# A two-layer streaming trunk on one core: the first wait of the value normalisation moved, a sixth norm buffer, and the last attention head reordered

## The chip, the cores and the metric

One core of one Trainium2 chip. The time is device microseconds for one launch, as the median of several runs. One further execution was taken with the hardware profiler; every row below is from it.

## The reference

Two layers, each `h = x + RMSNorm_post(mixer(RMSNorm_pre(x)))`, over 1024 prompt tokens and 32 sample tokens (1056 together), width 1024, all in float32.

```python
def gmlp_branch(u, v, z, ws, bs, gv):                       # layer 0, branch A
    u = gelu(u)
    v = rmsnorm(gelu(v).reshape(b, L, 4, 256), gv)          # per token and group of 256
    s = einsum('gij,bcjgk->bcigk', masked(ws), v chunks of 128) + bs
    return silu(z) * u * s, v
# layer 0, branch B: a Mamba-2 SSD scan over 16 heads; its output is normalised too
# layer 0 out: concat(A, B) @ w_out (2048 x 1024)
def odd_layer(...):                                         # layer 1, attention, 8 heads of 128
    q, k, v, z, f_logit = split(h @ w_in)
    q, k = rmsnorm(q, gq), rmsnorm(k, gk)                   # per head, over its 128 features
    p = softmax(q @ k.T * scale + f_cum(q) - f_cum(k))      # causal; the sample rows also see 256 cached keys
    o = (silu(z) * (p @ v)) @ w_out                         # 1024 x 1024
    return x + rmsnorm(o, g_post)
```

## The kernel before

Activations are kept with features on the 128 partitions and tokens along the free axis, in three chunks of `CH` = 352. Every float32 product of the projections is made as three matrix products of split numbers: high x high, low x high, high x low. The high part is made by ScalarE (ACT: `split_high`, `out_high`), the low part is raw minus high, by GpSimd (POOL: `split_low`) or VectorE (DVE). TensorE (PE) works through one fixed list of products. All five queues are written out by hand and joined by semaphores (`S("name")`), so an engine does its list in order, and a wait at the head of a list holds all that stands behind it.

**Value tiles (layer 0, branch A).** `v_group(i)`, four times, projects two tiles of v, and turns them (transposes by PE) into banks `PB[3]` to `PB[7]`, and the sixth piece again into `PB[3]`, which is why PE there waits for `v_tok` from DVE's first copy out of `PB[3]`. DVE copies the six pieces to `V`, sums squares (`SQV`), normalises, and between adds up the squares of the SSD output `YB` in `RSY`. Ahead of the first of these, DVE waits for outputs of the scan to be stored by DMA (`ssd_stored`, `conv_stored`), clears part of `V` and `RSY`, and waits for the gains (`gv_in`).

**Attention (layer 1).** `turn_steps(t)` has 12 steps. In step i PE projects one chunk of head p = t + 1 (v, z, q, k in this order) and does a part of the attention of head t: `scores(i)`, `turn_probs(i-1)`, `values(i-2)` for query block i. DVE takes the row maximum with the bias (`sm`), ACT takes the exponential (`ex`), DVE divides (`pn`, written to `SB`), PE turns `SB`, ACT copies it to `PT`. The norms of q and k go by chunk n = 0 to 5 (three of q, three of k): POOL squares into `NRM`, ACT makes `NRMH`, DVE makes `NRML`, PE sums over partitions (`norm_sum`), DVE takes the mean (`n_ms`), ACT the inverse root (`inverse_root`), DVE multiplies (`norms`, `n_done`). `NRM` has five slots; chunk 5 uses slot 0 again (`NORM_SLOT`), so its squares wait for the norms of chunks 0 to 3.

**Last head.** `turn_steps(7, project=False)` has nothing left to project. Its steps carry products of the output projection instead (`fill(i)`): `FILL[i]` gives which group of three half rows and how many of the eight weight rows k, each with three products for each of the three half rows. Step 5 ends group 0, so that ACT then squares its three banks (`out_squares`) and DVE multiplies them by the gains (`out_gained`) and frees them; `fill(6)` starts group 1 in the same banks. Step 8 and `fill(9)` do the same for groups 1 and 2. k = 7 needs this head's own output, split by `last_head_high` (ACT) and `last_head_low` (DVE). Six of the output weights are loaded while it runs, into `WOR`, and split into `WOH` by ACT and `WOL` by POOL. After step 11 nine more half rows follow.

Of the kernel before, what the change touches and what calls it, by code (L numbers as in the profile page):

```python
# [2550 lines left out]
```

## Time and profile before

| | us |
|---|---|
| median of 3 runs | 1603.23 (1602.16 to 1603.6) |
| the profiled execution | 1603.08 |
| its span, first to last instruction | 1601.1 |
| PE busy in the span | 1546.9 |
| DVE, ACT, POOL busy | 794.6, 676.4, 442.3 |

PE is the engine that is nearly always busy; 54 us of the span are not covered by its matrix products. A time in a row is counted from the start of the span. A busy PE need not run at full speed: the granted clock is shown beside it in views by stretch, 1.00 being 2.4 GHz and 0.50 being 1.2 GHz.

### The profile page before, as it was taken

How to read it: one execution, taken by the hardware profiler on the slowest of the kernel's cores; microseconds unless marked ns; L12 is line 12 of the kernel's file. 1: busy time of each engine (PE TensorE's matmuls, PEld its weight loads, DVE VectorE, ACT ScalarE, POOL GpSimd, SP SyncE). 2: the span in 40 equal slices, each digit the busy share in tenths (PEclk: the TensorE clock that was granted, in tenths of full speed). 3: DMA queues.
4: the chain of work that ended last, by engine and by line, in shares of the span. 5: the costliest groups of instructions: out<-in, count | busy, mean ns of one | idle time of the engine just before them, and what ended most of it. 6: DMA issues, size and time to landing. Idle time of an engine off the chain costs nothing.

```text
span 1601.1 us, 26475 instructions
## 1 busy us (share of the span) xinstructions
PE 1546.9 (97%) x9472; PEld 1420.5 (89%) x9472; DVE 794.6 (50%) x1750; ACT 676.4 (42%) x1258; POOL 442.3 (28%) x269
## 2 busy tenths in 40 slices
PE   6999999998999999999999999999999999998898
PEld 5999999998999999988888898989889898986676
DVE  5546777776784232436565243434434343435432
ACT  6434444442233323335455344545444544445321
POOL 1214544452221112244442312222222121316000
PEclk9999999999999999999999999999999999999999
DMA  4122122203112111244555644724232332213121
GB/s 152 42 69 72 60 87 74 71 33 83 52 27 56 40 39 39 95 168 157 171 189 110 76 64 41 73 40 70 40 70 44 59 60 43 60 43 139 54 95 70
DMA packets 129510, 121.09 MB, mean 76 GB/s; under 512 B 10291, under 2 KB 113293, under 8 KB 129453
## 3 DMA queue, kind: packets, MB, share of 16 engines
q1 hardware_dynamic: 129452, 120.32, 31.0%
q8 instruction: 37, 0.61, 0.2%
q14 instruction: 21, 0.16, 0.0%
HBM read 101.64 MB, written 18.66 MB: 75 GB/s over the span
## 4 chain that ended last, share of the span: by engine, by line
PE 83%; DVE 5%; ACT 4%; issue 4%; DMA 2%; POOL 1%; SPq 0%; ACTq 0%; POOLq 0%; DVEq 0%
PE PB L747 78%; PE PB L751 5%; DVE NRML L1914 2%; DMA XT<-in_x_prompt_dram 1%; DMA WRAW<-in_w_in_odd_dram 1%; ACT L1328 1%; ACT L1793 1%; DVE SB L1918 0%; ACT SB L1877 0%; ACT PT L1322 0%; ACT NRMH L1322 0%; ACT SQJ L1362 0%; POOL WL L627 0%; DVE KALL L1921 0%; DVE XT L1921 0%
## 5 line engine op out<-in xcount | busy, mean ns | idle before, releaser
L747 PE MATMUL PB<-HH,WH 128*128 128x352 f32 x1872 | 619.5, 331 | 2.5 <-DVE HL L1914 1.6
L747 PE MATMUL PB<-HH,WL 128*128 128x352 f32 x1872 | 602.7, 322 | 0.0
L747 PE MATMUL PB<-HL,WH 128*128 128x352 f32 x1872 | 602.0, 322 | 0.0
L747 PEld LDWEIGHTS PB<-HH,WH 128*128 128x128 f32 x1872 | 352.8, 188 | 19.5 <-issue 12.5
L747 PEld LDWEIGHTS PB<-HL,WH 128*128 128x128 f32 x1872 | 353.9, 189 | 0.2
L747 PEld LDWEIGHTS PB<-HH,WL 128*128 128x128 f32 x1872 | 352.5, 188 | 0.0
L627 POOL TENSOR_TENSOR WL<-WRAW,WH 128x1024 fp32r<-128x1024 f32 x82 | 201.6, 2459 | 542.7 <-ACT WH L1322 536.0
L1322 ACT ACTIVATE WH<-WRAW 128x1024 fp32r<-128x1024 f32 x112 | 118.0, 1053 | 16.2 <-DMA WRAW<-in_w_out_even_dram 8.0
L1877 ACT ACTIVATE SB<-SB,small 128x128 f32<-128x128 f32 (+8 forms) x72 | 53.8, 748 | 80.0 <-DVE small L1918 80.0
L1914 DVE TENSOR_TENSOR Y<-PB,Y 128x128 f32 (+2 forms) x72 | 20.2, 280 | 133.1 <-PE PB L747 133.1
L747 PE MATMUL PB<-PT,VTOK 128*128 128x128 f32 (+2 forms) x624 | 81.6, 274 | 0.1
L747 PEld LDWEIGHTS PB<-PT,VTOK 128*128 128x128 f32 (+1 forms) x624 | 78.2, 191 | 1.6 <-issue 0.2
L747 PE MATMUL PB<-KALL,QT 128*128 128x512 f32 (+4 forms) x208 | 78.6, 485 | 0.0
L1914 DVE TENSOR_TENSOR NRML<-NRM,NRMH 128x352 fp32r<-128x352 f32 x48 | 47.2, 983 | 57.2 <-ACT NRMH L1322 57.2
L655 POOL TENSOR_TENSOR M<-M,CBT 128x512 f32<-128x512 f32 (+1 forms) x48 | 62.2, 1322 | 47.5 <-ACT M L1511 47.5
L747 PE MATMUL PB<-WH,YSH 128*128 128x512 f32 x192 | 75.1, 391 | 0.0
L747 PE MATMUL PB<-WL,YSH 128*128 128x512 f32 x192 | 74.8, 389 | 0.0
L1322 ACT ACTIVATE PT<-PB 128x512 f32<-128x512 f32 (+3 forms) x112 | 45.7, 446 | 62.4 <-PE PB L751 62.3
L679 POOL TENSOR_TENSOR WL<-WRAW,WH 128x512 fp32r<-128x512 f32 x30 | 53.5, 1785 | 63.1 <-ACT WH L1322 63.1
L747 PE MATMUL PB<-WH,YSL 128*128 128x512 f32 x172 | 66.9, 389 | 0.0
L1914 DVE TENSOR_TENSOR UG<-UG,ZG 128x1056 f32<-128x1056 f32 x8 | 12.2, 1528 | 105.5 <-ACT ZG L1342 105.5
L2420 DVE CUSTOM_DVE_ANT_0 SB<-PB,NFB 128x512 f32<-128x512 f32 (+4 forms) x104 | 54.5, 547 | 14.9 <-PE PB L751 7.7
(312 smaller groups left out, 2338.0 us busy)
## 6 DMA issues: line engine op xcount, KB each, us to landing
WRAW<-in_w_out_even_dram SPq DMA_DIRECT2D x48, 512.0 KB, 3.6
WRAW<-in_w_in_even_dram SPq DMA_DIRECT2D x44, 512.0 KB, 3.8
WRAW<-in_w_in_odd_dram SPq DMA_DIRECT2D x32, 512.0 KB, 8.0
ACSB<-acs_rows SPq DMA_DIRECT2D x16, 528.0 KB, 5.3
NFB<-nf_rows SPq DMA_DIRECT2D x8, 656.0 KB, 3.9
XS<-in_x_prompt_dram SPq DMA_DIRECT2D x8, 512.0 KB, 6.4
XT<-in_x_prompt_dram SPq DMA_DIRECT2D x8, 512.0 KB, 5.3
x_rows<-OG SPq DMA_DIRECT2D x8, 512.0 KB, 5.7
```

Source lines behind the costliest of these rows:

```text
L627: pool.tensor_tensor(WL[:, slot(w), :, :], WRAW[:, slot(w), :, :], WH[:, slot(w), :, :].bitcast(f32), ALU.subtract).then_inc(S("w_low"), 1)
L655: pool.tensor_tensor(m, m, CBT[0:rows, g, b0:b0 + nb, 0:rows], ALU.mult).then_inc(S("m"), 1)
L679: pool.tensor_tensor(WLS[SLOT3[u % 3]][:, HALF:D], raw[:, HALF:D], WHS[SLOT3[u % 3]][:, HALF:D].bitcast(f32), ALU.subtract).then_inc(S("w_ ...
L747: return pe.matmul(out, lhsT, rhs, start=start, stop=stop)
L751: return pe.transpose(out, in_, IDENT[0:n, 0:n])
L1322: return act.activation(out, in_, ACT.Copy, scale=scale)
L1328: act.add_instruction(mybir.InstLoadActFuncSet(name=nc.get_next_instruction_name(), act_func_set_id=LN_EXP_SET, ins=[], outs=[]))
L1793: act.activation(Y1[:, p, :], Y1[:, p, :], ACT.Silu).then_inc(S("zs"), 1)
L1877: act.activation(SB[0:rows, 0:width], SB[0:rows, 0:width], ACT.Exp, scale=SCALE, bias=NBIAS[0:rows, :], accum_out=RSUM[0:rows, :]).then_in ...
L1914: return dve.tensor_tensor(out, a, b, op)
L2420: order(dve.tensor_tensor_reduce(SB[0:rows, c0:c1], PB[3 + k][0:rows, 0:c1 - c0], NFB[0:rows, key0 + c0:key0 + c1], 1.0, -3.0e38, ALU.add, ...
```

## The change

Nothing that is computed changes, and no product is added or taken away. There are three parts.

1. On DVE, ahead of the first value group: the waits for the stored outputs and the clearing of `RSY` move behind that group's sums of squares, and the wait for the gains stands just ahead of their first use. What is left ahead of the copies is the wait for `yb` and the clearing of part of `V`. The loop over the groups is partly written out.
2. `NRM` and `NRML` get a sixth slot, which lies over `KC` (the cached keys), so the squares of chunk 5 wait for `kc_turn` (PE's turn of `KC`, step 10). In step 9 PE's `norm_sum` of chunk 2 stands behind `values`. In step 10 ACT's `NRMH` copy stands ahead of the inverse root.
3. In the last head `fill` leads every step; the last head's output is split one step earlier; in steps 5 and 8 ACT's three squares stand ahead of the exponential, and DVE's first two gains and the mean stand ahead of the maximum of the scores, the third ahead of the division. The low part of the second output weight is made by DVE, not POOL. POOL makes three low parts of `WOL`, waits for the norms of head 7 (`n_done` 16), makes the low part of head 6, and then the other three.

```diff
-    NRM = r("NRM", [P, 5, CH])
-    NRML = at("NRML", c_phase, [P, 5, CH], f32r)
+    KC = at("KC", c_phase + 5 * CH * 4, [P, 2, P])
+    KSAM = KC[0:DEC, 0, :]
+    NRM = r("NRM", [P, 6, CH])
+    NRML = at("NRML", c_phase, [P, 6, CH], f32r)
...
-    NORM_SLOT = (0, 1, 2, 3, 4, 0)
...
-        def turn_parts(p):
+        def turn_parts(p, last=False):
...
                 if n == 5:
-                    pool.wait_ge(S("n_done"), 2 * p + 1)
+                    pool.wait_ge(S("kc_turn"), p + 1)
                 for cols, src in norm_chunk(n):
-                    last = pool.tensor_tensor(NRM[:, NORM_SLOT[n], cols], src, src, ALU.mult)
+                    last = pool.tensor_tensor(NRM[:, n, cols], src, src, ALU.mult)
                 last.then_inc(S("n_sq"), 1)
...
-            split_low(tile_no(W_QKVZ + 4 + Z_, 4, p))
+            if not last:
+                split_low(tile_no(W_QKVZ + 4 + Z_, 4, p))
 
         turn_parts(0)
-        with pool.Fori(1, 8) as p:
-            turn_parts(p)
-            pool.wait_ge(S("y1_hi"), p)
-            pool.tensor_tensor(YL[:, p - 1, :], Y1[:, p - 1, :], YH[:, p - 1, :].bitcast(f32), ALU.subtract) \
+        def low_of_head(h):
+
+            pool.wait_ge(S("y1_hi"), h + 1)
+            pool.tensor_tensor(YL[:, h, :], Y1[:, h, :], YH[:, h, :].bitcast(f32), ALU.subtract) \
                 .then_inc(S("y1_lo"), 1)
-        for k in range(2, 8):
+
+        def out_low(k):
+
             pool.wait_ge(S("w_high"), W_OO + k + 1)
             pool.tensor_tensor(WOL[:, k - 2, :], WOR[:, k - 2, :], WOH[:, k - 2, :].bitcast(f32),
                                ALU.subtract).then_inc(S("w_low"), 1)
-            if k == 7:
-                pool.wait_ge(S("n_done"), 16)
-                pool.wait_ge(S("y1_lo"), 7)
-                pool.tensor_copy(YSAM[:, 0:7, 0:DEC], YH[:, 0:7, SEQ:TOK]).then_inc(S("ysam"), 1)
-                pool.tensor_copy(YSAM[:, 0:7, DEC:2 * DEC], YL[:, 0:7, SEQ:TOK]).then_inc(S("ysam"), 1)
+
+        with pool.Fori(1, 7) as p:
+            turn_parts(p)
+            low_of_head(p - 1)
+        turn_parts(7, last=True)
+        pool.wait_ge(S("w_low"), W_OO + 2)
+        for k in range(2, 5):
+            out_low(k)
+        pool.wait_ge(S("n_done"), 16)
+        low_of_head(6)
+        for k in range(5, 8):
+            out_low(k)
+        pool.wait_ge(S("y1_lo"), 7)
+        pool.tensor_copy(YSAM[:, 0:7, 0:DEC], YH[:, 0:7, SEQ:TOK]).then_inc(S("ysam"), 1)
+        pool.tensor_copy(YSAM[:, 0:7, DEC:2 * DEC], YL[:, 0:7, SEQ:TOK]).then_inc(S("ysam"), 1)
...
-                if not project and i not in (6, 9):
+                if not project:
...
@@ -1272,8 +1284,6 @@
                 if project and i == 9:
                     pe.wait_ge(S("n_ms"), 6 * p + 1)
                     norm_sum(p, 1, 4)
-                    wait(pe, "pt_read", 13 * t + 12)
-                    norm_sum(p, 2, 6)
                 if project and i == 10:
                     pe.wait_ge(S("n_ms"), 6 * p + 3)
...
                 if attend and 2 <= i <= NB + 2:
                     values(t, i - 2)
+                if project and i == 9:
+                    wait(pe, "pt_read", 13 * t + 12)
+                    norm_sum(p, 2, 6)
...
-                if not project and i in (6, 9):
-                    fill(i)
...
-                if project and i == 10:
-                    act.wait_ge(S("n_ms"), 6 * p + 4)
-                    inverse_root(NRM[:, 0:4, :], "n_rt")
...
                     act.wait_ge(S("n_sq"), 6 * p + n + 1)
-                    copy(NRMH[:, n % 3, :], NRM[:, NORM_SLOT[n], :]).then_inc(S("n_hi"), 1)
+                    copy(NRMH[:, n % 3, :], NRM[:, n, :]).then_inc(S("n_hi"), 1)
+                if project and i == 10:
+                    act.wait_ge(S("n_ms"), 6 * p + 4)
+                    inverse_root(NRM[:, 0:4, :], "n_rt")
+                if not project and 2 <= i <= NB + 2:
+                    last_head_high(i - 2)
+                if not project and i in (5, 8):
+                    for h in range(i - 5, i - 2):
+                        out_squares(h)
...
-                if not project and i >= 3:
-                    last_head_high(i - 3)
                 if not project and i == 5:
-                    for h in range(0, 3):
-                        out_squares(h)
                     out_root(0)
                 if not project and i == 8:
-                    for h in range(3, 6):
-                        out_squares(h)
...
-        dve.wait_ge(S("cso"), 1)
-        dve.wait_ge(S("ssd_stored"), 256)
-        dve.wait_ge(S("conv_stored"), 96)
         dve.wait_ge(S("yb"), 8)
         order(dve.memset(V[:, :, NB * P:], 0.0))
-        order(dve.memset(RSY[:, :, :], 0.0))
-        order.fence()
-        dve.wait_ge(S("gv_in"), 48)
...
+        order.fence()
+
+        def value_norm(i, g, first=False):
+            for j in range(2):
+                for q, (b0, nb, rows) in enumerate(QUADS):
+                    bank = (3, 4, 5, 6, 7, 3)[3 * j + q]
+                    dve.wait_ge(S("v_turn"), 6 * i + 3 * j + q + 1)
+                    dve.tensor_copy(V[0:rows, 2 * i + j, b0 * P:(b0 + nb) * P], PB[bank][0:rows, 0:nb * P]) \
+                        .then_inc(S("v_tok"), 1)
...
+            ts(GSM[:, 2, 0:9], GSM[:, 0, 0:9], 1.0 / (2 * P), EPS, ALU.mult, ALU.add).then_inc(S("v_ms"), 1)
+
+            if first:
+                dve.wait_ge(S("cso"), 1)
+                dve.wait_ge(S("ssd_stored"), 256)
+                dve.wait_ge(S("conv_stored"), 96)
+                order(dve.memset(RSY[:, :, :], 0.0))
                 order.fence()
...
+                tt(RSY[:, g, :], RSY[:, g, :], TMP[:, :], ALU.add).then_inc(S("y_sq"), 1)
+                dve.wait_ge(S("y_sq"), 2 * i + j + 1)
+            dve.wait_ge(S("v_rt"), i + 1)
+            order(dve.reciprocal(GSM[:, 3, 0:9], GSM[:, 2, 0:9]))
...
+            if first:
+                dve.wait_ge(S("gv_in"), 48)
+            order(tt(vj[0], vj[0], GVB[:, i, 0:P].unsqueeze(1).broadcast_to([P, 9, P]), ALU.mult))
...
+        value_norm(0, 0, first=True)
+        value_norm(1, 0)
+        with order.loop(2, 4, 9) as i:
+            value_norm(i, 1)
...
+                if not project and i in (5, 8):
+                    out_gained(i - 5)
+                    out_gained(i - 4)
+                    out_mean((i - 5) // 3)
...
                 if project and i == 11:
                     norms(p, (0, 1, 2, 3), 1)
                     mean_square(p, 4, 4)
+                    if last:
+                        dve.wait_ge(S("w_high"), W_OO + 2)
+                        dve.wait_ge(S("p_chunk"), 3 * W_OO)
+                        tt(WL[:, 1, :, :], WRAW[:, 1, :, :], WH[:, 1, :, :].bitcast(f32), ALU.subtract) \
+                            .then_inc(S("w_low"), 1)
...
+                if not project and 2 <= i <= NB + 2:
+                    last_head_low(i - 2)
+                if not project and i in (5, 8):
+                    out_gained(i - 3)
...
-                if not project and i >= 3:
-                    last_head_low(i - 3)
-                if not project and i == 5:
-                    for h in range(0, 3):
-                        out_gained(h)
-                    out_mean(0)
...
                 if not project and i == 8:
-                    for h in range(3, 6):
-                        out_gained(h)
-                    out_mean(1)
...
-        with order.loop(0, 7, 40) as t:
+        with order.loop(0, 6, 40) as t:
             turn_steps(t)
+        turn_steps(6, last=True)
         turn_steps(7, project=False)
```

DVE at the start of the value tiles. `V`, `SQV`, `RSY`, `GSM` are as above, `TMP` is a square of `YB`; `XW` is the last work of the scan. Before, first piece (the register rows of the loop are part of it):

```order
L1921 SCALAR_TENSOR_TENSOR XW<-XC,DCOL,XW 128x32
L2115 MEMSET V 128x8x128
L2116 MEMSET RSY 128x2112
L95 UNCONDITIONAL_BRANCH
L95 ISA
L2125 ISA
L2125 COPY V<-PB 128x512
```

Now:

```order
L1931 SCALAR_TENSOR_TENSOR XW<-XC,DCOL,XW 128x32
L2122 MEMSET V 128x8x128
L2130 COPY V<-PB 128x512 x2
L2130 COPY V<-PB 32x128
L2130 COPY V<-PB 128x512 x2
L2130 COPY V<-PB 32x128
L1924 TENSOR_TENSOR SQV<-V 128x9x128 x2
L2137 TENSOR_REDUCE GSM<-SQV 128x9
L1927 TENSOR_SCALAR GSM<-GSM 128x9
L2145 MEMSET RSY 128x2112
L1924 TENSOR_TENSOR TMP<-YB 128x1056
```

The clearing of `RSY` stood between `V` and the first copy, and now stands behind the mean of the squares.

POOL from the end of the last turn's squares to its end. `WL` is the low part of a weight tile, `WOL` that of an output weight, `YL` that of a head's output. Before:

```order
L705 TENSOR_TENSOR NRM<-KALL 128x352 x2
L703 REGISTER_ALU
L705 TENSOR_TENSOR NRM<-KALL 128x320
L705 TENSOR_TENSOR NRM<-KALL 128x32
L624 REGISTER_ALU
L626 REGISTER_ALU
L627 TENSOR_TENSOR WL<-WRAW,WH 128x1024
L721 ISA
L721 TENSOR_TENSOR YL<-Y_134,YH 128x1056
L718 REGISTER_ALU
L718 COMPARE_AND_BRANCH
L725 TENSOR_TENSOR WOL<-WOR,WOH 128x1024 x6
```

Now:

```order
L704 TENSOR_TENSOR NRM<-KALL 128x352 x2
L704 TENSOR_TENSOR NRM<-KALL 128x320
L704 TENSOR_TENSOR NRM<-KALL 128x32
L727 TENSOR_TENSOR WOL<-WOR,WOH 128x1024 x3
L721 TENSOR_TENSOR YL<-Y_134,YH 128x1056
L727 TENSOR_TENSOR WOL<-WOR,WOH 128x1024 x3
```

One `WL` split has gone (to DVE), and `YL` stands between the two halves of the `WOL` splits.

ACT in steps 4 to 6 of the last head: `SB` 128x640 is the exponential of step 4, 128x768 that of step 5; `JUNKF` are the three output squares; `YH` is the high part of this head's output. Before:

```order
L1877 ACTIVATE SB,small<-SB,small 128x640
L1322 ACTIVATE YH<-Y_134 128x128
L1322 ACTIVATE PT<-PB 128x512
L1322 ACTIVATE PT<-PB 128x128
L1877 ACTIVATE SB,small<-SB,small 128x768
L1322 ACTIVATE YH<-Y_134 128x128
L1754 ACTIVATE JUNKF,small<-PB 128x512 x3
```

Now:

```order
L1893 ACTIVATE SB,small<-SB,small 128x640
L1333 ACTIVATE PT<-PB 128x512
L1333 ACTIVATE PT<-PB 128x128
L1333 ACTIVATE YH<-Y_134 128x128
L1765 ACTIVATE JUNKF,small<-PB 128x512 x3
L1893 ACTIVATE SB,small<-SB,small 128x768
```

The three squares and one `YH` copy stood behind the exponential of step 5 and stand ahead of it.

## Rows read from the trace of the kernel before

**Rows 1.** The page: its span and the row of PE.

```profile
span 1601.1 us, 26475 instructions
...
PE 1546.9 (97%) x9472; PEld 1420.5 (89%) x9472; DVE 794.6 (50%) x1750; ACT 676.4 (42%) x1258; POOL 442.3 (28%) x269
```

**Rows 2.** PE in time order: start, us, engine, line, form, count, [idle before, releaser].

```profile
374.55 1.15 PE L751 MATMUL PB<-IDENT,VG 128*128 128x128 f32 x9
...
382.62 0.40 PE L751 MATMUL PB<-IDENT,UG 128*32 128x128 f32 x1 [6.05 <-DVE V L2125]
```

**Rows 3.** The same view of DVE, first to third value group.

```profile
377.06 0.91 DVE L2115 MEMSET V<- 128x1024 f32 x1 [12.30 <-DMA out_dram<-CSO]
378.36 1.82 DVE L2116 MEMSET RSY<- 128x2112 f32 x1 [0.39 <-issue]
381.87 2.87 DVE L2125 COPY V<-PB 128x512 f32 x6 [1.69 <-DMA WS<-in_gmlp_ws_dram]
...
408.68 2.87 DVE L2125 COPY V<-PB 128x512 f32 x6 [5.32 <-PE PB L751]
...
417.20 1.26 DVE L1914 TENSOR_TENSOR TMP<-YB 128x1056 f32 x1
...
433.74 2.87 DVE L2125 COPY V<-PB 128x512 f32 x6 [3.09 <-PE PB L751]
```

**Rows 4.** The same view of POOL: the last gate of the scan.

```profile
364.83 2.46 POOL L660 TENSOR_TENSOR YB<-YB,XW 128x1056 f32<-128x1056 f32 x1 [6.81 <-DVE XW L1921]
```

**Rows 5.** Stretches: length, PE busy (instructions), granted clock, DMA share, GB/s.

```profile
382.00:388.00 6.00, 5.38 (x21) 0.58 0.18 48
1462.00:1466.00 4.00, 3.75 (x10) 0.57 1.02 413
1478.00:1484.00 6.00, 4.91 (x16) 0.72 0.00 0
1498.00:1506.00 8.00, 5.74 (x30) 1.00 0.00 0
```

**Rows 6.** Waits of PE in 1000 to 1460 us: total, times, longest.

```profile
PE PB L747 <- DVE NRML L1914: 2.9, 12, 0.3
```

**Rows 7.** Waits of PE in 900 to 1000 us, first row.

```profile
PE PB L747 <- DVE NRML L1914: 0.8, 3, 0.5
```

**Rows 8.** DVE in time order: `NRML` of chunk 5, head 6 to 7.

```profile
1384.90 2.17 DVE L1914 TENSOR_TENSOR NRML<-NRM,NRMH 128x352 fp32r<-128x352 f32 x1 [1.13 <-ACT NRMH L1322]
```

**Rows 9.** Waits of PE from 1460 us to the end, the four longest.

```profile
PE PB L751 <- DVE SB L1918: 3.4, 2, 2.3
PE PB L751 <- DVE KALL L1921: 2.7, 1, 2.7
PE PB L747 <- DVE NRML L1914: 2.3, 1, 2.3
PE PB L747 <- DVE YL L1914: 2.0, 1, 2.0
```

**Rows 10.** A DVE and a POOL instruction side by side, last head.

```profile
1471.41 2.70 POOL L725 TENSOR_TENSOR WOL<-WOR,WOH 128x1024 fp32r<-128x1024 f32 x1
...
1471.76 2.70 DVE L1921 SCALAR_TENSOR_TENSOR KALL<-KALL,COLS,NRM 128x320 f32<-128x320 f32 x1
```

**Rows 11.** ACT, DVE and PE in time order, last head, steps 5 to 7.

```profile
1500.17 0.58 ACT L1754 ACTIVATE JUNKF<-PB 128x512 f32<-128x512 f32 x1
...
1500.93 0.60 ACT L1754 ACTIVATE JUNKF<-PB 128x512 f32<-128x512 f32 x1
...
1501.03 2.09 DVE L1914 TENSOR_TENSOR FOG<-PB,POSTF 128x512 f32<-128x512 f32 x3
...
1500.97 0.87 PE L751 MATMUL PB<-IDENT,SB 128*128 128x128 f32 x6 [2.26 <-DVE SB L1918]
...
1507.47 0.39 PE L747 MATMUL PB<-WOH,YH 128*128 128x512 f32 x1
...
1513.71 1.50 PE L747 MATMUL PB<-PT,VTOK 128*128 128x128 f32 x12
```

More of the change, by code:

```diff
@@ L1127, in norm_sum @@
             mm(PB[bank][:, 0:CH], ONESR[:, :], NRMH[:, n % 3, :], stop=False)
-            mm(PB[bank][:, 0:CH], ONESR[:, :], NRML[:, NORM_SLOT[n], :], start=False).then_inc(S("n_ss"), 1)
+            mm(PB[bank][:, 0:CH], ONESR[:, :], NRML[:, n, :], start=False).then_inc(S("n_ss"), 1)
         def turn_quad(src, q, bank, sem):
@@ L2108, in _ @@
         pair_steps(8, project=False)
-        dve.wait_ge(S("cso"), 1)
-        dve.wait_ge(S("ssd_stored"), 256)
-        dve.wait_ge(S("conv_stored"), 96)
         dve.wait_ge(S("yb"), 8)
         order(dve.memset(V[:, :, NB * P:], 0.0))
-        order(dve.memset(RSY[:, :, :], 0.0))
         order.fence()
-        dve.wait_ge(S("gv_in"), 48)
-        for g in range(GROUPS_B):
-            with order.loop(2 * g, 2 * g + 2, 9) as i:
-                for j in range(2):
-                    for q, (b0, nb, rows) in enumerate(QUADS):
-                        bank = (3, 4, 5, 6, 7, 3)[3 * j + q]
-                        dve.wait_ge(S("v_turn"), 6 * i + 3 * j + q + 1)
-                        dve.tensor_copy(V[0:rows, 2 * i + j, b0 * P:(b0 + nb) * P], PB[bank][0:rows, 0:nb * P]) \
-                            .then_inc(S("v_tok"), 1)
-                dve.wait_ge(S("v_tok"), 6 * i + 6)
-                vj = [V[:, 2 * i + j, :].rearrange("p (b f) -> p b f", f=P) for j in range(2)]
-                for j in range(2):
-                    order(tt(SQV[:, :, j * P:(j + 1) * P], vj[j], vj[j], ALU.mult))
+        def value_norm(i, g, first=False):
[5 more added lines that the diff above has]
+                        .then_inc(S("v_tok"), 1)
+            dve.wait_ge(S("v_tok"), 6 * i + 6)
+            vj = [V[:, 2 * i + j, :].rearrange("p (b f) -> p b f", f=P) for j in range(2)]
+            for j in range(2):
+                order(tt(SQV[:, :, j * P:(j + 1) * P], vj[j], vj[j], ALU.mult))
+            order.fence()
+            order(dve.tensor_reduce(GSM[:, 0, 0:9], SQV[:, :, :], AX.X, ALU.add))
+            order.fence()
+            ts(GSM[:, 2, 0:9], GSM[:, 0, 0:9], 1.0 / (2 * P), EPS, ALU.mult, ALU.add).then_inc(S("v_ms"), 1)
[4 more added lines that the diff above has]
+                order(dve.memset(RSY[:, :, :], 0.0))
@@ L2131, in _ @@
                 order.fence()
-                order(dve.tensor_reduce(GSM[:, 0, 0:9], SQV[:, :, :], AX.X, ALU.add))
+            for j in range(2):
+                yb = YB[:, 2 * i + j, :]
+                order(tt(TMP[:, :], yb, yb, ALU.mult))
                 order.fence()
-                ts(GSM[:, 2, 0:9], GSM[:, 0, 0:9], 1.0 / (2 * P), EPS, ALU.mult, ALU.add).then_inc(S("v_ms"), 1)
-                for j in range(2):
-                    yb = YB[:, 2 * i + j, :]
-                    order(tt(TMP[:, :], yb, yb, ALU.mult))
-                    order.fence()
-                    tt(RSY[:, g, :], RSY[:, g, :], TMP[:, :], ALU.add).then_inc(S("y_sq"), 1)
-                    dve.wait_ge(S("y_sq"), 2 * i + j + 1)
@@ new lines, in value_norm @@
+                dve.wait_ge(S("y_sq"), 2 * i + j + 1)
+            dve.wait_ge(S("v_rt"), i + 1)
+            order(dve.reciprocal(GSM[:, 3, 0:9], GSM[:, 2, 0:9]))
+            order.fence()
+            for j in range(2):
+                order(tt(vj[j], vj[j], GSM[:, 3, 0:9].unsqueeze(2).broadcast_to([P, 9, P]), ALU.mult))
+            order.fence()
+            if first:
+                dve.wait_ge(S("gv_in"), 48)
+            order(tt(vj[0], vj[0], GVB[:, i, 0:P].unsqueeze(1).broadcast_to([P, 9, P]), ALU.mult))
@@ L2152, in _ @@
+            order.fence()
+            tt(vj[1], vj[1], GVB[:, i, P:2 * P].unsqueeze(1).broadcast_to([P, 9, P]), ALU.mult) \
+                .then_inc(S("v_normed"), 1)
+        value_norm(0, 0, first=True)
+        value_norm(1, 0)
+        with order.loop(2, 4, 9) as i:
+            value_norm(i, 1)
         dve.wait_ge(S("ws_turn"), 1)
@@ L2381, in _, with turn_steps @@
         dve.wait_ge(S("lf_stored"), 32)
-        def turn_steps(t, attend=True, project=True):
+        def turn_steps(t, attend=True, project=True, last=False):
             p = t + 1
@@ L2395, in norms @@
                     for cols, x in norm_chunk(n):
-                        last = stt(x, x, COLS[:, gain:gain + 1], NRM[:, NORM_SLOT[n], cols], ALU.mult, ALU.mult)
+                        last = stt(x, x, COLS[:, gain:gain + 1], NRM[:, n, cols], ALU.mult, ALU.mult)
                 last.then_inc(S("n_done"), 1)
```

18 lines of the change are left out of this document (3 added, 15 removed).

## The prediction, made before the changed kernel had run

> **What bounds it now.** I read the page first: PE is busy 1546.9 of 1601.1 us [rows 1], so only its 54 idle us and its stretches at a lower clock can be won. Then PE's waits, stretch by stretch, and around each the instructions of all engines in time order. Three places belong to the change. At the first value group PE stands 6.05 us on a DVE copy [rows 2], and the granted clock of the six us behind it is 0.58 on average [rows 5]. In the attention loop PE waits 12 times, 2.9 us in all, on `NRML` [rows 6], and 0.8 us before that [rows 7]. In the last head the four longest groups of waits make 3.4 + 2.7 + 2.3 + 2.0 = 10.4 us [rows 9], and two stretches run at 0.57 and 0.72 of full clock [rows 5]. The rest of PE's idle time (start, between the layers, end) isn't touched. The sum is made against the profiled execution, 1603.1 us with 1601.1 in the span; it stands 0.1 under the median of 1603.2.
>
> **Part 1, the value tiles.** PE begins to turn the first group at 374.55 and stops at 376.57 for DVE's first copy [rows 2]. DVE was free but stood 12.3 us until 377.06, when the stored convolution rows landed; then came 0.91 and 1.82 us of clearing and 1.69 of waiting for the gains, and the copy began at 381.87 [rows 3]. Now DVE needs only `yb`, POOL's last gate, which ends at 364.83 + 2.46 = 367.3 [rows 4]; the 0.9 of clearing `V` is over by 368.3. The first copy runs at 375.1, half a us long, and PE does not stop. Won: 6.05 us, and the clock. Six us at 0.58 lose 6 x 0.42 = 2.5, part of it while PE was still idle; from first copy to first copy the group takes 408.68 - 381.87 = 26.8 against 433.74 - 408.68 = 25.1 next [rows 3], which says 1.7. I take 2.0.
>
> What is late next? DVE. Its first group has 25.1 - 3.1 = 22.0 us of work [rows 3] plus 1.8 for `RSY`, from 375.1 to about 399.2. PE brings the next piece 25 us after the first, at 400. So about 1 us of slack covers the moved clearing. The stored rows (landed 377.06) and the gains (381.87) are wanted only after 384 and 390. Without that slack the cost would be at most the 1.8 of the clearing. Part 1: -8.0, bounds -6.2 and -8.6.
>
> **Part 2, the loop.** Chunk 5's squares stood behind the norms of chunks 0 to 3; they now need only ACT's copy of the last k chunk, about 2 us earlier. ACT's high part stands behind a weight split and a copy on its own queue, so it gains some 1.5 us, and so does `NRML`. Per turn PE waited 0.30 there and 0.16 for chunk 2, whose sum now stands behind 2 us of `values`. These are the 12 + 3 waits: -3.7 in all; I take -3.5. The new wait for `kc_turn` is met a step earlier and costs nothing.
>
> What can go wrong is the port. `NRML` of chunk 5, 352 wide, took 2.17 us [rows 8], where a 1056-wide product takes 1.26 [rows 3]. The side-by-side rows show why: DVE's product, ready at 1471.76, ended at 1474.46, after POOL's split ended at 1474.11, and that split took 2.70 instead of 2.4 [rows 10]. A DVE instruction with both inputs in SBUF thus sits out the POOL instruction under way, and gets in at its end, ahead of POOL's next. With the squares earlier, POOL starts its split (2.4 us) about a us earlier too, among DVE's norms. If DVE gets in at each boundary, `NRML` ends at about 1386.2; it ended at 1387.1 [rows 8] with PE waiting 0.3, so PE wants it at 1386.8: no wait.
> The Trainium skill (SBUF — State Buffer, Who interferes with whom) says the shared port pair is locked for a whole instruction by whichever issues first, and the other fully blocks. The trace agrees on the blocking; on who wins a boundary the page says nothing further, and by issue order alone it could be POOL, which is the second rival below.
>
> **Part 3, the last head.** Removed: the 10.4 us of waits, and the low clock: 4 x 0.43 + 6 x 0.28 = 3.4 [rows 5]. Together 13.8.
> Against it stand new waits. I lay the instructions of the four queues out by their durations in the rows, from PE's last projection (1455.9) on:
> - Steps 0 to 2. DVE makes the second weight's low part after the norms: about 1.25 us (no such row on DVE; a 1056-wide product from SBUF takes 1.26 [rows 3]; not under 0.7, not over 3.7 if a POOL split must be sat out). `NRML` of chunk 5 follows it and is ready at 1460.2; PE has been there since 1459.6: 0.6. The first `WOL` ends at 1463.3, its `WOR` tile having just landed: 0.5, and 0.1 for the third.
> - Steps 2 and 3. POOL stands until head 7's norms are done (about 1469.3), so those run without a split beside them: the 2.7 of waiting on `KALL` goes. But then come `YL` and three splits, 2.4 to 2.7 each [rows 10]. `SB` of step 1 must sit out `YL`: PE waits 0.9. The k = 5 low part is ready at 1474.8, PE is there at 1473.4: 1.4. `SB` of step 2 sits out a split: 0.4.
> - Step 5: k = 7 needs the split output of block 1, now a step earlier; the 2.0 goes and nothing comes.
> - Steps 5 and 6. `fill(6)` now leads, and covers the 2.26 of waiting for `SB` [rows 11]. But it needs its banks back. Let F be the end of `fill(5)`. Values, transposes and scores take PE to F + 2.8. ACT copies `PT` until F + 2.3, the output's high part 0.2, then squares three banks 0.76 apart (1500.17, 1500.93 [rows 11]); DVE's gains take 0.7 each (2.09 for three [rows 11]). The first bank is free at F + 4.0: PE waits 1.2. The third gain stands behind the softmax chain of step 5 (1.4 us) and ends at F + 7.2: PE, after two trios of 0.7 (27 products from 1507.47 to 1513.71, 0.23 each [rows 11]), waits 1.8.
> - Steps 8 and 9 repeat this with longer `PT` copies: 2.0 and 1.2.
> The new waits make 1.2 + 2.7 + 3.0 + 3.2 = 10.1. So part 3 is -13.8 + 10.1 = -3.7. Small waits that the four groups leave out (under 0.4 each) go too, so I take -4.5. Bounds: 0 if each of the two places at steps 6 and 9 brings back a low clock (1.7 each, as above) and the weight's low part takes 3.7 (2.5 more, less what overlaps); -7 if ACT and DVE run the squares closer than I think.
>
> Sum: -8.0 - 3.5 - 4.5 = -16.0, so 1603.2 - 16.0 = 1587.2 us.
>
> **The rivals.**
> 1. The reordered last head gives nothing: its waits move from `SB` and `KALL` to the output banks, and the clock falls there as it did at 1478. For it: PE is busy only 1.4 of 4.5 us around `fill(6)`, and the waits of 2.7 and 1.1 before 1480 left a clock of 0.72 behind them [rows 5, 9]. Against: the wait of 2.26 that ends at 1500.97 [rows 11] left it at 1.00 [rows 5]. Then 1603.2 - 8.0 - 3.5 = 1591.7.
> 2. POOL wins each boundary of the port. Then split and `YL` run back to back, the norms of chunks 2 and 3 and `NRML` of chunk 5 sit out both (2.4 + 2.7), and PE waits 2.6 us or more in each of 8 turns: +21, with part 1 -8.0 and the last head at best -2: about 1614. It decides the sign from 1.6 us a turn on (8.0 + 4.5 over 8). Against it stand three products in a row that each got in, one of which is in [rows 10].
> 3. Part 1 does not do what it says: DVE is late for the second group or `V` can't be cleared early, and the 6 us come back as another wait on the same copies. Then about 1595. The idle 12.3 us of DVE ahead of the copy [rows 3] speak against it.
> 4. Nothing measurable: parts 1 and 3 both give their gain back. It would need a new wait on PE of 12 us that no queue above shows.
>
> **Chances.** Forecast, all three parts work in kind: 0.80, its own range 1583 to 1590.5. Rival 1: 0.09. Rival 3: 0.05. Rival 2: 0.04. Rival 4: 0.02. Within 0.2% (3.2 us) a measurement of this kernel can't tell a change from none. The range 1582 to 1594.5 takes in the forecast with the bounds of parts 1 and 3 and rival 1. Faster by over 0.2%: 0.94; within: 0.02; slower: 0.04.
>
> **What would show it.** Part 1: no wait of PE on `V`, clock 1.00 from 376 to 400, DVE idle before its second group about 1 us instead of 5.3. Part 2: no wait on `NRML` in 1000 to 1440 or under 0.1 each; a wait on `SB` of 0.2 per turn stays. Part 3: PE waits on `FOG` at `fill(6)` and `fill(9)`, 1 to 2 us each, on `WOL` at step 3, none on `KALL`; the stretch from the last projection to the last `PT` product 3 to 6 us shorter. Wrong if PE waits on `NRML` or `QT` each turn, if the clock falls at `fill(6)` and `fill(9)`, or if a wait on `V` stays.

## The result and the profile after

The changed kernel takes 1576.34 us (median of 4 runs, 1575.39 to 1579.82) against 1603.27 for before (4 runs): ratio 0.9839, 95% interval 0.9826 to 0.9853. It is 26.9 us faster, and 10.9 us faster than predicted; 1576.3 lies below the range. The profiled execution took 1575.49, with 1573.8 in the span, 27.3 less than before.

The page of the changed kernel, beside [rows 1]:

```profile
span 1573.8 us, 26349 instructions
...
PE 1534.6 (98%) x9472; PEld 1415.8 (90%) x9472; DVE 794.0 (50%) x1751; ACT 677.1 (43%) x1258; POOL 444.7 (28%) x268
```

PE's busy time fell by 12.3 us and its idle time from 54.2 to 39.2, by 15.0. The products are the same, so the fall of the busy time needs a reason: a product at a low clock is busy for longer (the mean granted clock went from 0.995 to 0.999), and short waits that the view hides count as busy too, as shown below.

DVE in time order in the value tiles, beside [rows 3]:

```profile
367.03 0.91 DVE L2122 MEMSET V<- 128x1024 f32 x1 [2.81 <-POOL YB L659]
...
374.84 2.87 DVE L2130 COPY V<-PB 128x512 f32<-128x512 f32 x6 [6.89 <-PE PB L763]
...
399.63 2.87 DVE L2130 COPY V<-PB 128x512 f32<-128x512 f32 x6 [0.87 <-PE PB L763]
```

DVE now stands ready for PE at the first copy (it was PE that stood for DVE), and the idle time ahead of the second group is 0.87 us, where the prediction said about 1.

PE's waits in 980 to 1430 us, the loop (beside [rows 6]), the whole answer:

```profile
PE PB L763 <- DVE SB L1928: 1.3, 6, 0.2
```

PE's waits in 1435 to 1520 us, the last head (beside [rows 9]), the whole answer:

```profile
PE PB L759 <- ACT JUNKF L1765: 2.5, 2, 1.6
PE PB L759 <- issue: 2.0, 2, 1.3
PE PB L759 <- POOL WOL L727: 1.6, 2, 1.1
PE PB L759 <- DVE NRML L1924: 0.5, 1, 0.5
```

The four old groups of 10.4 us are gone but for 0.5 on `NRML`. What stands there now is 6.6 us, at the places that the prediction named. PE in time order has the starts; only rows with idle time are copied:

```profile
1440.39 0.40 PE L759 MATMUL PB<-NRMH,ONESR 128*128 128x352 f32 x1 [0.48 <-DVE NRML L1924]
...
1443.58 0.50 PE L759 MATMUL PB<-WOH,YH 128*128 128x512 f32 x1 [0.52 <-POOL WOL L727]
...
1454.21 0.50 PE L759 MATMUL PB<-WOH,YH 128*128 128x512 f32 x1 [1.06 <-POOL WOL L727]
...
1469.09 0.47 PE L759 MATMUL PB<-WH,YH 128*128 128x512 f32 x1 [0.94 <-ACT JUNKF L1765]
...
1472.13 0.47 PE L759 MATMUL PB<-WH,YH 128*128 128x512 f32 x1 [1.33 <-issue]
```

At `fill(6)` the second wait carries no name ("issue"). DVE's row of the third gain gives it: it ends at 1471.35 + 0.68 = 1472.03, and PE goes on at 1472.13.

```profile
1471.35 0.68 DVE L1924 TENSOR_TENSOR FOG<-PB,POSTF 128x512 f32<-128x512 f32 x1
```

The clock did not fall. Stretches, columns as in [rows 5]:

```profile
1466.00:1476.00 10.00, 7.69 (x37) 5.60 (x38) 4.63 (x15) 4.24 (x13) 0.00 (x0) 1.00 0.00 0
1476.00:1498.00 22.00, 22.00 (x117) 17.16 (x115) 7.33 (x24) 5.62 (x13) 0.00 (x0) 1.00 0.14 49
```

### Where the 27 us went: starts, not idle times

To share out the gain I took the same three instructions in each trace and compared their starts: POOL's first square of q of each turn (`NRM<-QT`; the first one ends the part before the loop, the eighth begins the last head), and the last `PT,VTOK` group on PE. "Turn" is the distance from the second to the eighth of those squares, divided by six. All in us and from one profiled execution each; the experiments below stand in the same table. What follows the last `PT,VTOK` is 60.2 us in every row.

| kernel | before the loop | turn | last head | span |
|---|---|---|---|---|
| before | 911.28 | 75.12 | 119.51 | 1601.1 |
| after | 901.92 | 73.51 | 111.63 | 1573.8 |
| e1 part 1 | 902.15 | 75.10 | 118.14 | 1590.6 |
| e2 part 2 | 912.05 | 73.53 | 116.46 | 1588.8 |
| e3 part 3 | 911.34 | 75.07 | 114.11 | 1595.6 |
| e4 ACT's order | 910.00 | 74.32 | 121.17 | 1596.7 |
| e5 slot alone | 912.15 | 77.64 | 115.41 | 1612.7 |
| e6 sum behind values | 910.44 | 74.70 | 121.57 | 1600.0 |
| e7 third gain | 902.10 | 73.51 | 109.20 | 1571.6 |
| e8 three edits | 904.19 | 73.52 | 106.84 | 1571.3 |
| e9 slot, split held | 910.44 | 74.79 | 119.25 | 1597.5 |
| e10 after, root first | 902.51 | 76.98 | 111.50 | 1595.2 |
| e11 gain and low part | 902.60 | 73.51 | 109.06 | 1571.8 |

After against before: 9.36 before the loop, 10.15 from first to eighth square (0.50 in the first turn, which has no attention, and 6 x 1.61), 7.88 in the last head: 27.4. The prediction had 8.0, 3.5 and 4.5 for the three parts. The size is off in the loop above all: 1.61 us a turn, where the view of waits had shown 0.46 (0.30 + 0.16).

The six turns and the last head as stretches, columns as in [rows 5] with the other engines between. Before:

```profile
970.78:1421.47 450.69, 445.73 (x2834) 407.10 (x2832) 186.57 (x595) 215.00 (x420) 103.49 (x72) 1.00 0.35 56
1421.47:1540.98 119.51, 107.85 (x574) 87.51 (x573) 53.52 (x148) 45.78 (x104) 27.62 (x18) 0.97 0.20 71
```

After:

```profile
960.92:1401.96 441.04, 439.77 (x2834) 407.09 (x2832) 187.26 (x595) 215.89 (x420) 107.09 (x72) 1.00 0.35 57
1401.96:1513.58 111.62, 104.67 (x575) 85.30 (x574) 51.27 (x150) 46.04 (x104) 25.71 (x17) 1.00 0.21 74
```

In the loop the granted clock is 1.00 in both, so it has no share in the 9.65 us of the six turns; 3.7 of them are idle time of PE and 6.0 are time that the view had called busy. In the last head 4.7 are idle time and 3.2 busy time, and there the clock tells the busy part: before has two stretches at 0.50 (1462 to 1466, 1479 to 1483), which lose 3.4 us by [rows 5], and after has none.

What the view hides in the loop can be seen from starts. PE in time order around the sum of chunk 4, before:

```profile
1380.68 0.60 PE L751 MATMUL PB<-IDENT,VRAW 128*128 128x128 f32 x4
1381.40 0.43 PE L747 MATMUL PB<-NRMH,ONESR 128*128 128x352 f32 x1
1381.67 0.32 PE L747 MATMUL PB<-NRML,ONESR 128*128 128x352 f32 x1
1381.98 0.43 PE L747 MATMUL PB<-HH,WH 128*128 128x352 f32 x1
```

and after:

```profile
1362.39 0.60 PE L763 MATMUL PB<-IDENT,VRAW 128*128 128x128 f32 x4
1362.75 0.41 PE L759 MATMUL PB<-NRMH,ONESR 128*128 128x352 f32 x1
1363.00 0.33 PE L759 MATMUL PB<-NRML,ONESR 128*128 128x352 f32 x1
1363.16 0.32 PE L759 MATMUL PB<-HH,WH 128*128 128x352 f32 x1
```

No row of either bears an idle time. Yet from the turn of `VRAW` to the sum it was 0.72 us and is 0.36, and from `NRML` to the next projection 0.31 and now 0.16. Matmuls overlap, and the view counts idle time from the modelled end of the one before (0.60 us after its start, where the next may follow at 0.36). So a wait of a third of a us shows as nothing here. Over a whole turn (the third of the six), the starts of PE's products in before and after draw apart at three places, and by less than 0.06 us a step everywhere else: 0.44 net around chunk 2, 0.6 at chunk 4 and 0.5 at chunk 5.

### The profile page after: what moved, and what is told of

Same layout as the page of the kernel before. It is cut to its first block, busy times and chain, and to the rows that moved or that the text cites. A ratio compares the mean times of both kernels' runs of the same rounds, so it can differ in the third digit from the quotient of the medians.

```text
span 1573.8 us, 26349 instructions
## 1 busy us (share of the span) xinstructions
PE 1534.6 (98%) x9472; PEld 1415.8 (90%) x9472; DVE 794.0 (50%) x1751; ACT 677.1 (43%) x1258; POOL 444.7 (28%) x268
## 4 chain that ended last, share of the span: by engine, by line
PE 88%; ACT 4%; DVE 3%; issue 3%; DMA 1%; POOL 1%; SPq 0%; ACTq 0%; DVEq 0%; POOLq 0%
PE PB L759 83%; PE PB L763 5%; DMA XT<-in_x_prompt_dram 1%; ACT L1339 1%; ACT L1804 1%; ACT SB L1893 0%; ACT SQJ L1373 0%; DVE XT L1931 0%; DMA WOR<-in_w_out_odd_dram 0%; DVE SB L1928 0%; ACT WH L1333 0%; POOL WL L626 0%; DMA XS<-in_x_prompt_dram 0%; DVE XS L1928 0%; DVE M L1931 0%
## 5 line engine op out<-in xcount | busy, mean ns | idle before, releaser
L759 PEld LDWEIGHTS PB<-HH,WH 128*128 128x128 f32 x1872 | 351.9, 188 | 17.5 <-issue 10.4
L1924 DVE TENSOR_TENSOR Y<-PB,Y 128x128 f32 (+3 forms) x72 | 20.2, 281 | 127.6 <-PE PB L759 127.5
L704 POOL TENSOR_TENSOR NRM<-QT 128x352 f32<-128x352 f32 x24 | 20.0, 832 | 147.9 <-ACT QT L1333 147.9
```

The source lines that it names most:

```text
L704: last = pool.tensor_tensor(NRM[:, n, cols], src, src, ALU.mult)
L759: return pe.matmul(out, lhsT, rhs, start=start, stop=stop)
L1924: return dve.tensor_tensor(out, a, b, op)
```

## The experiments

Two theories at the start. **A:** the waits of the loop are as long as the start-to-start distances say; part 2 is worth 10.5 to 12 us, one line of it (ACT's order) 4 us by itself, and the three parts add up. **B:** the idle times of the view are right; part 2 is worth 3.5 to 4, and the rest came from elsewhere or from the parts acting together.

### e1, e2, e3: each part alone

e1 is before with the first value group as in the change. e2 is before with the sixth slot, the sum of chunk 2 behind `values`, and ACT's new order in step 10. e3 is before with the last head's changes.

```diff
# e1
+            if first:
+                dve.wait_ge(S("cso"), 1)
+                dve.wait_ge(S("ssd_stored"), 256)
+                dve.wait_ge(S("conv_stored"), 96)
+                order(dve.memset(RSY[:, :, :], 0.0))
...
# e2
-    NORM_SLOT = (0, 1, 2, 3, 4, 0)
+    NORM_SLOT = (0, 1, 2, 3, 4, 5)
...
# e3
-                if not project and i not in (6, 9):
+                if not project:
...
```

Expected of e1: 

> Part 1 alone on the kernel before. Both theories: the copies out of the first bank come at once, so 8.5 us less than before (the loop and the last head keep their lengths). If part 1 is where more than predicted was won, it is 12 us or more less; if parts need each other, under 6.

Measured: 1593.39, ratio 0.9941 (0.9928 to 0.9955). Before the loop 9.13 us less, the turns unchanged, the last head 1.4 shorter though its code is that of before: PE's wait on `KALL` there was 1.1 instead of 2.7. So the last head can differ by some such amount between kernels that have it alike.

Expected of e2: 

> Part 2 alone (sixth slot, the sum of chunk 2 behind values, ACT's NRMH copy ahead of the inverse root). Theory A, waits counted from start to start (a turn 1.57 us shorter, seven turns, plus the last one): 10.5 to 12 us less than before. Theory B, idle time as the view of waits gives it: 3.5 to 4 less, and the rest of the gain came from parts 1 or 3 or only with them.

Measured: 1593.94, ratio 0.9941 (0.9927 to 0.9954), that is 9.5 us. The turns are 1.59 shorter, the last head 3.05. PE's waits of e2 in 1440 to 1560 us:

```profile
...
PE PB L747 <- POOL WOL L725: 1.9, 1, 1.9
PE PB L747 <- DVE NRML L1915: 1.3, 1, 1.3
PE PB L751 <- DVE KALL L1922: 1.3, 1, 1.3
```

Against [rows 9] `NRML` and `KALL` give back 1.0 and 1.4; `WOL` has 1.9, where before had 0.3 in this stretch. The clock does the larger part of the 3.05: it falls once in this last head (1456 to 1460), where it fell twice in before, and each time loses 1.7 us. All this is from one execution, which was the fastest of e2's five (1590.86); at the median of 1593.94 the loop's 10 us alone make up the gain. Theory A; B would have had 1599.5.

Expected of e3: 

> Part 3 alone, with the loop of before. Theory A: 7.5 us less than before, all of it from the first VRAW group of the last head on, and the parts add up (8.5 + 11 + 7.5 = 27). Rival: part 3 gains only with the earlier norms of part 2, then 4 to 5 less.

Measured: 1597.08, ratio 0.9961 (0.9947 to 0.9975), 6.3 us; the interval (4.0 to 8.5 us) takes in both the 7.5 of theory A and the 4 to 5 of the rival. The last head is 5.40 shorter by itself, and 4.83 shorter on top of part 2 (116.46 to 111.63), so part 3's own share is about 5; part 2, put on top of it, brings the last head from 114.11 to 111.63. PE's granted clock is 1.00 in this last head too, but PE still waits 1.7 for `NRML` (0.5 in the changed kernel) and 2.2 for `WOL` (1.6). The parts add up: 0.9941 x 0.9941 x 0.9961 = 0.9844, the whole change 0.9839.

### e4 and e6: two lines of part 2, each alone

```diff
# e4: ACT, step 10
-                if project and i == 10:
-                    act.wait_ge(S("n_ms"), 6 * p + 4)
-                    inverse_root(NRM[:, 0:4, :], "n_rt")
...
+                if project and i == 10:
+                    act.wait_ge(S("n_ms"), 6 * p + 4)
+                    inverse_root(NRM[:, 0:4, :], "n_rt")
# e6: PE, step 9, behind values instead of ahead
-                    wait(pe, "pt_read", 13 * t + 12)
-                    norm_sum(p, 2, 6)
...
+                if project and i == 9:
+                    wait(pe, "pt_read", 13 * t + 12)
+                    norm_sum(p, 2, 6)
```

Expected of e4: 

> One line of part 2 alone: in step 10 ACT makes NRMH ahead of the inverse root. Theory A: the sum of chunk 4 stood late by 0.38 + 0.15 us in each turn though the view shows no wait there, so 3.5 to 4.3 us less than before. Theory B, which the prediction held: no wait there, no difference (under 0.5).

Measured: 1598.63, ratio 0.9969 (0.9958 to 0.9980), 5.0 us. A turn is 0.80 shorter: by the starts of PE's products in the third turn 0.63 at chunk 4 and 0.12 at chunk 5. PE's waits of e4 in 980 to 1430 us:

```profile
PE PB L747 <- DVE NRML L1914: 2.0, 12, 0.2
```

The view's total fell from 2.9 [rows 6] to 2.0, by 0.9, while the same six turns shortened by 6 x 0.80 = 4.8. This is the cleanest proof against theory B: a change that it priced at nothing gave 5 us. (This profile's last head was 1.7 longer than that of before, with the clock low three times instead of twice.)

Expected of e6: 

> The sum of chunk 2 behind values in step 9, alone. Theory A: start to start PE lost 0.33 to 0.43 us a turn there, so a turn 0.35 to 0.43 shorter, 2.5 to 3.2 us in all. Theory B (idle of the view, 0.16 a turn): 1.1 us in all.

Measured: 1601.84, ratio 0.9988 (0.9979 to 0.9997), 1.9 us: the time lies between the two theories. The turn decides: 0.42 shorter, 6 x 0.42 = 2.5 us in six turns, as A has it (the view's 0.16 would be 1.0); this profile's last head took 2.1 us more than that of before, of which 1.7 are a third fall of the clock (before has two) and the rest waits, on `KALL` (3.4 against 2.7) and `WOL` (1.9 against 0.3). That hides part of the gain in the time.

### e5: the sixth slot alone

```diff
...
-                    pool.wait_ge(S("n_done"), 2 * p + 1)
+                    pool.wait_ge(S("kc_turn"), p + 1)
...
```

Expected: 

> The sixth norm slot alone (squares of chunk 5 wait for kc_turn, ACT still makes the inverse root ahead of NRMH, the sum of chunk 2 where it was). Theory A, start to start: the rest of the 1.57 us of a turn after 0.76 for the ACT order and 0.43 for the sum of chunk 2, so 0.3 to 0.4 a turn, 2.5 to 3 us in all. Theory B, the prediction's: nearly all of part 2's gain is here (0.3 a turn by the view, up to 2.4 us), so its time alone says little, but then the turn must lose its wait on NRML of 0.3 at chunk 5. Rival, the port: an earlier split pushes the norms and a turn gets longer.

Measured: 1615.31, ratio 1.0078 (1.0063 to 1.0092): 12 us slower. Both theories missed it, and the rival on the port has it. It is the blocking of the prediction's second rival, though not under its condition, as shown further down. POOL of e5 in time order:

```profile
1394.13 1.33 POOL L705 TENSOR_TENSOR NRM<-KALL 128x320 f32<-128x320 f32 x2 [4.64 <-ACT KALL L1322]
1395.43 2.70 POOL L627 TENSOR_TENSOR WL<-WRAW,WH 128x1024 fp32r<-128x1024 f32 x1
1398.08 2.70 POOL L721 TENSOR_TENSOR YL<-Y,YH  x1
```

and DVE of e5 at the same time:

```profile
1393.83 2.04 DVE L1921 SCALAR_TENSOR_TENSOR QT<-QT,COLS,NRM 128x352 f32<-128x352 f32 x3
1395.79 2.72 DVE L1921 SCALAR_TENSOR_TENSOR KALL<-KALL,COLS,NRM 128x352 f32<-128x352 f32 x1
1398.43 0.51 DVE L1917 TENSOR_SCALAR NRM<-PB 128x352 f32<-128x352 f32 x1
1398.86 2.30 DVE L1914 TENSOR_TENSOR NRML<-NRM,NRMH 128x352 fp32r<-128x352 f32 x1
```

The norm of the last k chunk comes 0.36 us after the split has begun and ends 0.38 after the split's end (1395.43 + 2.70 = 1398.13). POOL's `YL` has begun by then, at 1398.08. DVE's mean, whose input is in PSUM, takes 0.51 beside it; `NRML` of chunk 5 sits it out (ends 1401.16, `YL` at 1400.78). PE stands for it:

```profile
1401.22 0.43 PE L747 MATMUL PB<-NRMH,ONESR 128*128 128x352 f32 x1 [1.89 <-DVE NRML L1914]
```

A stretch of e5 behind this wait, columns as in [rows 5]:

```profile
1402.70:1405.90 3.20, 3.20 (x12) 3.20 (x12) 0.11 (x1) 0.00 (x0) 0.00 (x0) 0.50 0.10 30
```

So the wait costs twice: 1.5 us by itself (1.89 where before had 0.34 in the same place), and 3.2 us at 0.50 of full clock, 1.6 lost. The turns show both: the first two of the six are 76.6 us (wait only), the other four 78.2.

In the changed kernel the split comes just as early, without harm. Its POOL and its DVE in time order, the same place:

```profile
1363.28 1.53 POOL L704 TENSOR_TENSOR NRM<-KALL 128x320 f32<-128x320 f32 x2 [4.62 <-ACT KALL L1333]
1364.77 2.42 POOL L626 TENSOR_TENSOR WL<-WRAW,WH 128x1024 fp32r<-128x1024 f32 x1
```

```profile
1362.17 1.58 DVE L1931 SCALAR_TENSOR_TENSOR QT<-QT,COLS,NRM 128x352 f32<-128x352 f32 x3 [2.42 <-ACT NRM L1560]
1363.66 1.05 DVE L1931 SCALAR_TENSOR_TENSOR KALL<-KALL,COLS,NRM 128x352 f32<-128x352 f32 x1
1364.63 0.51 DVE L1927 TENSOR_SCALAR NRM<-PB 128x352 f32<-128x352 f32 x1
1365.37 2.20 DVE L1924 TENSOR_TENSOR NRML<-NRM,NRMH 128x352 fp32r<-128x352 f32 x1 [0.23 <-ACT NRMH L1333]
```

The norms begin 1.1 us ahead of the squares, not 0.3. The last one is done before the split holds the port; only `NRML` meets the split, and it gets in at its end (1367.57, the split at 1367.19). That is the prediction's picture. What it left out is what keeps it so: the norms start early because nothing else is between ACT's root and them. In e5 ACT's copy for chunk 4 stands behind the root, its `NRML` ahead of the norms on DVE, and the norms are late.

### e9 and e10: is it the port, and is it ACT's order?

e9 is e5 with POOL's split held until the norms are done. e10 is after with ACT's order undone.

```diff
# e9, POOL, on top of e5
             for n in range(3, 6):
                 squares(n)
+            pool.wait_ge(S("n_done"), 2 * p + 1)
             split_low(tile_no(W_QKVZ + 4 + Z_, 4, p))
# e10, ACT, step 10
+                if project and i == 10:
+                    act.wait_ge(S("n_ms"), 6 * p + 4)
+                    inverse_root(NRM[:, 0:4, :], "n_rt")
...
-                if project and i == 10:
-                    act.wait_ge(S("n_ms"), 6 * p + 4)
-                    inverse_root(NRM[:, 0:4, :], "n_rt")
```

Expected of e9: 

> The slot alone again, but POOL's split of the z weight waits until the norms of chunks 0 to 3 are done (n_done), as the squares of chunk 5 did before. Theory port: the slot alone lost 11.6 us since the last k norm sat out that split (2.72 us) and NRML of chunk 5 then sat out YL (2.30), with PE waiting 1.9 for it. Held back, the norms run free, NRML sits out the split alone and ends about 2 us earlier: a turn of 75.1 us or less, a time of 1603 or less. Rival (the lateness comes from ACT's queue, not from POOL): a turn stays at 76.5 to 78.

Measured: 1600.61, ratio 0.9981 (0.9973 to 0.9990). One more wait made the kernel 14.7 us faster than e5 and 2.9 faster than before; a turn is 74.79. The norm of the last k chunk is free again and `NRML` sits out the split alone. DVE of e9:

```profile
1380.16 0.57 DVE L1922 SCALAR_TENSOR_TENSOR KALL<-KALL,COLS,NRM 128x352 f32<-128x352 f32 x1
...
1381.09 2.65 DVE L1915 TENSOR_TENSOR NRML<-NRM,NRMH 128x352 fp32r<-128x352 f32 x1
```

ACT's queue is that of e5, so the loss was POOL's instruction under way.

Expected of e10: 

> After, with the one line of part 2 undone: the inverse root ahead of NRMH again. If the gains of part 2's edits add up (0.76 us a turn for this one), about 1576.3 + 5.5 = 1582. If this edit is what keeps the sixth slot out of the port lock, as the loss of the slot alone says, a turn is 1.5 to 3 us longer than in the kernel with the other edit only, and the time is 1588 to 1600.

Measured: 1596.88, ratio 0.9957 (0.9944 to 0.9969): 20.5 us above after by the medians (19 by the ratios), for one edit to ACT's queue, of which about 5 is its own worth (e4) and the rest what it keeps away. Three of its six turns also have a stretch at 0.50 (77.7 us a turn, the other three 76.2). Its last head is as long as that of after (111.50 against 111.63), so ACT's order is not what part 2 does there. PE's waits of e10 in 980 to 1430 us:

```profile
PE PB L759 <- DVE NRML L1924: 11.3, 6, 1.9
```

The three edits of part 2 are thus worth, per turn: ACT's order 0.80, the sum behind `values` 0.42, and the slot 0.39 (1.61 less the other two) with them, but a loss of 2.5 without (e5). With the sum moved and ACT's order as before the slot still loses (e10, 76.98).

### e7, e8, e11: what the last head still held

```diff
# e7, DVE: the third gain ahead of the maximum of steps 5 and 8 too
                     out_gained(i - 4)
+                    out_gained(i - 3)
# e8: e7, fill(6) and fill(9) behind values, and on POOL
+        out_low(5)
         low_of_head(6)
-        for k in range(5, 8):
+        for k in range(6, 8):
# e11: e8 with the fills ahead, as in after
```

Expected of e7: 

> After, with DVE's third gain of steps 5 and 8 ahead of the maximum too. If the third bank's late gain is what PE stands for at fill(6) and fill(9) (1.33 and 0.71 by the view, 1.8 and 1.2 by the layout), the time is 2 to 3 us under after's, about 1573.9. Rival: the exponential is 0.7 us later for it and PE gets a wait on SB instead, then no difference.

Expected of e8: 

> After, with the third gain ahead, with fill(6) and fill(9) behind values as in before, and with the low part of weight row k = 5 ahead of head 6's YL on POOL. If the waits left in the last head are the output banks (1.2, 1.6) and WOL of k = 5 (1.06), the time is about 4 us under after's: 1572.3. Rival: the wait on SB of 2.26 and 1.1 us that the fills covered comes back, then it is no better than the kernel with the third gain alone, or 1 to 2 us worse.

Expected of e11: 

> After, with the third gain ahead of the maximum and the low part of weight row k = 5 ahead of head 6's YL, fills leading as in after. The third gain alone gave 1573.7. If WOL's 1.1 us is a wait that falls away whole: 1572.7; the fills behind values in the kernel with three edits then gave only 0.4. If the 1.4 us between those two came from the fills: 1573.7.

Measured, as ratio to before: e7 1573.66, 0.9817 (0.9804 to 0.9829); e8 1572.25, 0.9803 (0.9791 to 0.9816); e11 1573.66, 0.9810 (0.9797 to 0.9823). The third gain is what PE stood for under the name "issue": the rows of 1.33 and 0.71 are gone, the last head is 2.4 shorter, and the median is 2.7 lower than that of after, though the two intervals still touch (0.9829 and 0.9826). e11 shows where a wait goes that is pushed off. PE's waits of e11 in 1433 to 1560 us:

```profile
PE PB L760 <- ACT JUNKF L1766: 2.5, 2, 1.6
PE PB L764 <- DVE SB L1929: 1.1, 1, 1.1
...
PE PB L760 <- POOL WOL L727: 0.4, 1, 0.4
```

Against e7, `WOL` lost 1.0 (it had 1.4) and `SB` took 1.1: nothing won. In e8 the fills behind `values` take away the 2.5 of `JUNKF` as well; its waits in the same stretch:

```profile
PE PB L764 <- DVE SB L1931: 1.4, 2, 1.1
...
PE PB L760 <- POOL WOL L727: 0.3, 1, 0.3
```

By the table's measure its last head takes 106.84 us, e7's 109.20 and e11's 109.06; its medians gain only 1.4, and its part before the loop was 2.1 us longer in the profile (904.19 against 902.10) with the same code; 1.7 of that is a stretch at 0.50 from 888 to 893 that e7 does not have. The intervals of the three overlap, so their order is not shown. That e8 beats the changed kernel is: its interval ends at 0.9816, that of after begins at 0.9826.

## Why the prediction was too cautious

**The step that failed** is part 2's: "These are the 12 + 3 waits: -3.7 in all; I take -3.5." It measured -10.15 in the loop (e2 by ratio -9.5 in all). Two things in it were wrong. The price of each wait was the idle time of the view, 0.46 us a turn; start to start the same places held 1.61. And ACT's new order got no term, because the sum of chunk 4 shows no wait in the view; alone it gave 5.0 us (e4).

**Part 1** was right: -8.0 predicted, -9.13 in e1 before the loop and -9.5 by the ratio. Of the 1.1 over it, 0.5 lay ahead of the change, in the scan (its last product on DVE at 363.98 against 364.50). The slack of 1 us was 0.87.

**Part 3** was right in kind, and a term of its sum was too large: "The new waits make 1.2 + 2.7 + 3.0 + 3.2 = 10.1". They measured 6.6. The other side of the sum held: the four old waits went (but for 0.5 on `NRML`, which is counted in the 6.6), and the clock stayed at 1.00. With 6.6 in the place of 10.1 the sum is -13.8 + 6.6 = -7.2, against -7.88 in the table and -7.6 from the last projection to the last `PT` product, where the prediction said -4.5 and "3 to 6 us shorter". The last head is not part 3's alone: by itself part 3 gave 5.4 there (e3), and the waits on `NRML` and `WOL` fell as far as they did only with part 2. What part 2 does there, beyond these two waits, isn't taken apart.

Its new waits stood where they were laid out: 0.5 on `NRML` (0.6), 0.52 and 1.06 on `WOL` (0.5 and 1.4), 0.94 and 1.33 at `fill(6)` (1.2 and 1.8), at `fill(9)` 1.57 and 0.71 (2.0 and 1.2). The two waits on `SB` that had been forecast (0.9 and 0.4) didn't come, nor the 0.1 on the third `WOL`. It said "PE waits on `FOG`"; the profile writes `JUNKF` and "issue".

**The rivals.** Rival 1 (the last head gives nothing, the clock falls at `fill(6)`) is refuted by e3 and by the clock of 1.00, rival 3 by e1, and rival 4 by the size of the gain. Rival 2 did not come in the changed kernel, but its mechanism is real: e5 and e10. It was drawn with the wrong condition. It doesn't need POOL to win a boundary: in each meeting above DVE got in as soon as POOL's instruction ended. It needs the norms to be late by a us, so that two DVE products meet two POOL instructions. The prediction gave this rival 0.04 as a race between two engines; what it hangs on in the runs is one line of ACT's queue.

The Trainium skill (SBUF — State Buffer, Who interferes with whom) says that a VectorE instruction with two SBUF inputs contends with a GpSimd instruction that reads SBUF, and that the lock is exclusive: whoever issues first has it for the whole instruction, and the other blocks. The rows agree: 2.72 us for a product of 0.57, ended 0.38 after the split. They also show who goes next, which the page leaves open.

## What to carry to other kernels

Price a short wait on TensorE by the distance between starts, against the same pair of instructions where nothing waits, and not by the idle time shown: here the latter was under a third of it, and nothing at the place that was worth most. Long waits are another matter: in the last head the view's idle times and the granted clock gave a sum within 0.7 us of the time measured (7.2 and 7.88). An edit that makes one engine earlier can be a loss alone and a gain with another (the slot: +2.5 us a turn or -0.39); look for which instruction must come first, and test the edits apart and together. And where VectorE and GpSimd both work from SBUF, count the meetings: each VectorE product with both inputs in SBUF that began inside a long GpSimd instruction here lasted until 0.38 us after its end.

## What the runs showed of the hardware

- A wait of 1.89 us on PE left 3.2 us at a granted clock of 0.50 behind it in e5, while waits of 0.94 and 1.33 within 4 us left it at 1.00 in the changed kernel. The first two turns of e5 had the same wait of 1.89 and stayed at 1.00 (76.6 us a turn): it does not always bring the low clock. What decides stays open.
- The blocking goes both ways. POOL's split took 2.70 us in e5, where a DVE norm was under way as it began (the three `QT` norms end at 1395.87, the split begins at 1395.43), and 2.39 and 2.42 in e9 and after, where the norm had ended just before. A DVE product that came 0.12 us after the split's start (e9) didn't lengthen it.
- Part of the gain of an edit can be lost in a spread that is not its own. The last head whose steps are those of before took 118.1 (e1), 119.5 (before), 121.2 (e4) and 121.6 us (e6), with PE's wait on `KALL` between 1.1 and 3.4. The clock is the larger part of the step to e4 and e6: before has two stretches at 0.50 there, 3.4 us lost in all, and e4 and e6 have three, 5.1 lost.
